# Delta rule of a hybrid decoder layer: preparation inside the projection, samples and end as pipelines

## What is computed

```python
# x: 512 prompt tokens and 8 samples of one token; d_model 2048; p: weights
def token_mixers(h, st, p, pos0):
    proj = h @ p['w_in']                                   # 2048 x 6400
    pa, pb, pc, pd = jnp.split(proj, [A_COLS, A_COLS + B_COLS, A_COLS + B_COLS + C_COLS], axis=-1)
    a_b, a_c, a_h = jnp.split(pa, 3, axis=-1)              # group A: short gated convolution
    u_ext = jnp.concatenate([st_a, a_c * a_h], axis=1)
    y_a = a_b * causal_dwconv(u_ext, p['conv_a_w'])
    ...                                                    # group B: retention -> y_b
    prev = jnp.concatenate([st_shift[:, None, :], pc[:, :-1]], axis=1)   # group C: delta rule
    xs = pc + (prev - pc) * p['mu_c']
    r, kc, vc, wl, al, gl = jnp.split(xs, ..., axis=-1)
    w = -jax.nn.softplus(-(p['w0'] + jnp.tanh(wl) @ p['w2'])) - 0.5
    decay = jnp.exp(-jnp.exp(w))
    a = jax.nn.sigmoid(p['a0'] + al @ p['a2'])
    gate = jax.nn.sigmoid(gl) @ p['g2']
    kk = hs(kc * p['k_k'])                                 # hs: 8 heads of 64
    kk = kk / jnp.maximum(jnp.sqrt(jnp.sum(kk * kk, axis=-1, keepdims=True)), 1e-12)
    k4 = hs(kc * (1.0 + (a - 1.0) * p['k_a']))
    o_c, new_wkv = wkv7_scan(st_wkv, r4, hs(decay), k4, v4, kk, a4)
    o_c = layernorm_lastdim(o_c, RWKV_GN_EPS) * p['lnx_g'] + p['lnx_b']
    bonus = jnp.sum(r4 * k4 * p['r_k'], axis=-1, keepdims=True) * v4
    y_c = (o_c + bonus) * gate
    d1, d2 = jnp.split(pd, 2, axis=-1)                     # group D: 31 taps, norm, swish
    c = causal_dwconv(concat[st_d, d1 * jax.nn.sigmoid(d2)], p['conv_d_w']) + p['conv_d_b']
    y_d = jax.nn.silu(layernorm_lastdim(c, EPS) * p['ln_d_g'] + p['ln_d_b'])
    y = jnp.concatenate([y_a, y_b, y_c, y_d], axis=-1) @ p['w_out']
```

## Time and profile before

| | us |
|---|---|
| median of 3 runs | 3401.66 |
| lowest and highest of them | 3401.51, 3402.88 |
| the profiled execution | 3402.08 |
| its span | 3400.3 |
| busy in the span: PE, DVE, ACT, POOL | 3176.2, 1144.5, 823.6, 1263.9 |

### The profile page before, as it was taken

How to read it: one execution, slowest core, us unless ns; L and a number is a source line. 1 busy time by engine, 2 the same in 40 slices (tenths; PEclk the granted TensorE clock), 3 DMA queues, 4 the chain that set the end, 5 groups by cost and what they waited for, 6 DMA issues and landing times.

```text
span 3400.3 us, 63387 instructions
## 1 busy us (share of the span) xinstructions
PE 3176.2 (93%) x28930; PEld 3083.9 (91%) x28930; DVE 1144.5 (34%) x1355; ACT 823.6 (24%) x1034; POOL 1263.9 (37%) x520
## 2 busy tenths in 40 slices
PE   6999999999259789999989999999999999999997
PEld 6999999999128679978889999999999999999997
DVE  6417873342756542312322311212121111111123
ACT  5431121222102222311212322222122222222221
POOL 6864444333100024322134344444444444444442
PEclk9999999999579899999999999999999999999998
DMA  6663423223000022366542222222222222222222
GB/s 236 214 188 94 120 80 124 93 94 119 24 15 4 4 104 90 112 206 209 180 160 90 87 92 90 93 94 94 93 89 93 93 94 94 90 91 94 94 94 76
DMA packets 147867, 357.57 MB, mean 105 GB/s; under 512 B 24592, under 2 KB 75024, under 8 KB 145296
## 3 DMA queue, kind: packets, MB, share of 16 engines
q1 hardware_dynamic: 109904, 312.58, 27.6%
q10 hardware_dynamic: 37696, 40.94, 3.8%
HBM read 332.34 MB, written 21.13 MB: 104 GB/s over the span
## 4 chain that ended last, share of the span: by engine, by line
PE 92%; DVE 5%; DMA 1%; ACT 1%; issue 0%; ACTq 0%; SPq 0%; POOL 0%; DVEq 0%
PE gp L1400 81%; PE gp L861 1%; PE mp L861 1%; PE mp L853 1%; PE mp L1201 1%; PE gp L1447 1%; PE mp L1184 1%; DMA work<-in_cache_k 0%; PE mp L1232 0%; PE mp L1213 0%; DVE work L972 0%; DVE work L289 0%; DVE work L997 0%; DVE work L1070 0%; DVE work L1854 0%
## 5 line engine op out<-in xcount | busy, mean ns | idle before, releaser
L1380 POOL TENSOR_TENSOR lo<-raw,hi 128x1024 fp32r<-128x1024 f32 x516 | 1263.7, 2452 | 2093.8 <-ACT hi L1517 2093.4
L1400 PE MATMUL gp<-xh,hi 128*128 128x260 f32 x5120 | 1457.5, 285 | 11.4 <-DVE xl L1777 8.6
L1400 PE MATMUL gp<-xh,lo 128*128 128x260 f32 x5120 | 1450.2, 283 | 0.0
L1400 PE MATMUL gp<-xl,hi 128*128 128x260 f32 x5120 | 1445.9, 282 | 0.0
L1517 ACT ACTIVATE hi<-raw 128x1024 fp32r<-128x1024 f32 x516 | 546.6, 1060 | 2096.0 <-PE gp L1400 2048.1
L1400 PEld LDWEIGHTS gp<-xh,hi 128*128 128x128 f32 x5120 | 967.7, 189 | 22.2 <-issue 18.8
L1400 PEld LDWEIGHTS gp<-xl,hi 128*128 128x128 f32 x5120 | 966.8, 189 | 0.5
L1400 PEld LDWEIGHTS gp<-xh,lo 128*128 128x128 f32 x5120 | 966.9, 189 | 0.0
L1400 PE MATMUL gp<-uh,lo 128*128 128x260 f32 x2048 | 578.7, 283 | 0.0
L1400 PE MATMUL gp<-uh,hi 128*128 128x260 f32 x2048 | 578.3, 282 | 0.0
L1400 PE MATMUL gp<-ul,hi 128*128 128x260 f32 x2048 | 576.6, 282 | 0.0
(11 more groups left out here) (299 smaller groups left out, 2103.2 us busy)
## 6 DMA issues: line engine op xcount, KB each, us to landing
raw<-in_w_up SPq DMA_DIRECT2D x128, 512.0 KB, 3.3
raw<-in_w_down SPq DMA_DIRECT2D x128, 512.0 KB, 3.3
raw<-in_w_in SPq DMA_DIRECT2D x100, 512.0 KB, 3.3
raw<-in_w_k SPq DMA_DIRECT2D x32, 512.0 KB, 3.5
raw<-in_w_v SPq DMA_DIRECT2D x32, 512.0 KB, 4.1
raw<-in_w_out SPq DMA_DIRECT2D x32, 512.0 KB, 3.3
raw<-in_w_q SPq DMA_DIRECT2D x32, 512.0 KB, 5.4
work<-in_cache_k SPq DMA_DIRECT2D x32, 512.0 KB, 6.6
```

The lines of the kernel that those rows point to most:

```text
L1380: nc.gpsimd.tensor_tensor(lo[:, s, :], raw[:, s, :], hi[:, s, :].bitcast(F32), ALU.subtract).then_inc(lo_ready, 1)
L1400: last = nc.tensor.matmul(gp[:, par, h, 0:c1 - c0], w, m[:, c0:c1], start=a, stop=b)
```

## The change

What is moved, added and taken out:

- The order of the tiles: D stays in 0 to 7; then half of A (two channel tiles) in 8 to 13, r and v in 14 to 21, B in 22 to 37, tiles 12, 13 and k of C in 38 to 43, and the other half of A in 44 to 49.
- The token shift is made tile by tile behind its eviction (`c_shift`), in place, with a copy of the last columns into a small buffer `c_last`, from which the state output is stored. r and v are stored shifted.
- The d taps go nine to a tile instead of eight; the samples' part of D goes to units 36 and 37, the norm's mean to 38, its centring to 39, variance 40, scaling 41, product 43. Retention's constants are loaded in one go at unit 44.
- Small products of C go to units 82 to 85, unit-length keys to 88 to 94, decays to 92, keys to 95 to 98. Exclusive decays are no longer computed apart: they are the running ones read one column to the left (`g_sh`), and the third exponential falls away.
- r and v are loaded again, with the samples' states, behind the last unit.
- Samples: two operand buffers and both sets of banks are used in turn, and vector n + 2 is built behind the use of vector n.
- Chunk loop: in its first four rounds each channel tile's bonus is made, with two matmuls in bank set z and four DVE operations; it goes into Y. The loop's scratch stands from column 8T on, in one piece.
- End: no shared norm function; the four tiles' means, variances and roots run in two sets of banks in turn, and scale and bias with the bonus are one operation.

```diff
-D_S, R_S, A_S, B_S, K_S = 0, 8, 16, 28, 44
+D_S, A_S, R_S, B_S, K_S, E_S = 0, 8, 14, 22, 38, 44
 SLOTS = [D0 + GT * (1 - n % 2) + n // 2 for n in range(ND_T)]
+SLOTS += [A0 + GT * ((n + 1) % 3) + n // 3 for n in range(NA_T // 2)]
 SLOTS += [C0 + n for n in (0, 1, 2, 3, 8, 9, 10, 11)]
-SLOTS += [A0 + GT * ((n + 1) % 3) + n // 3 for n in range(NA_T)]
 SLOTS += [B0 + GT * (n % 4) + n // 4 for n in range(NB_T)]
-SLOTS += [C0 + n for n in (4, 5, 6, 7, 12, 13)]
+SLOTS += [C0 + n for n in (12, 13, 4, 5, 6, 7)]
+SLOTS += [A0 + GT * ((n + 1) % 3) + n // 3 for n in range(NA_T // 2, NA_T)]
...
+        def c_shift(dve, x, c, n):
...
+            if n >= 2:
+                dve.wait_ge(S("c_shifted"), n - 1)
+            V.tensor_copy(c_last[:, c, :], x[:, NP - 1:]).then_inc(S("c_diff"), 1)
+            V.tensor_tensor(d[:, 1:NP], x[:, 0:NP - 1], x[:, 1:NP], ALU.subtract).then_inc(S("c_diff"), 1)
+            V.tensor_scalar(d[:, 0:1], x[:, 0:1], -1.0, None, ALU.mult).then_inc(S("c_diff"), 1)
+            V.tensor_tensor(d[:, NP:], c_sh[:, c, :], x[:, NP:], ALU.subtract).then_inc(S("c_diff"), 1)
+            dve.wait_ge(S("c_diff"), 4 * (n + 1))
+            V.scalar_tensor_tensor(out=x, in0=d, scalar=pr("mu_c", c), in1=x, op0=ALU.mult, op1=ALU.add).then_inc(S("c_shifted"), 1)
...
+        def c_square(dve, lane, j):
...
+            dve.wait_ge(S("c_shifted"), 8 + 2 + j + 1)
+            lane.done(nc.vector.tensor_scalar(c_kk[:, j, :], c_k[:, j, :], pr("k_k", j), None, ALU.mult))
+            lane.tell(nc.vector.tensor_tensor(c_d[:, j % 2, :], c_kk[:, j, :], c_kk[:, j, :], ALU.mult), S("c_kksq"), j + 1)
...
+            dve.wait_ge(S("c_kkn"), j + 1)
+            lane.done(nc.vector.tensor_scalar(d, d, 1e-12, None, ALU.max))
+            lane.done(nc.vector.reciprocal(d, d))
+            nc.vector.tensor_tensor(c_kk[:, j, :], c_kk[:, j, :], d, ALU.mult).then_inc(S("c_unit"), 1)
...
+            lane.done(nc.vector.tensor_scalar(d, c_a[:, j, :], -1.0, pr("k_a", j), ALU.add, ALU.mult))
+            lane.done(nc.vector.scalar_tensor_tensor(out=c_k[:, j, :], in0=d, scalar=1.0, in1=c_k[:, j, :], op0=ALU.add, op1=ALU.mult))
+            lane.tell(nc.vector.tensor_tensor(c_a[:, j, :], c_a[:, j, :], c_kk[:, j, :], ALU.mult), S("c_vectors"), j + 1)
...
-            if u == 41:
+            if u == 38:
                 d_mean(pe)
...
                 b_pe(pe, h, step)
+            if 82 <= u < 86:
+                c_lora(pe, u - 82)
+            if 89 <= u < 93:
+                c_norm(pe, u - 89)
...
+            if u % 2 == 0 and R_S < u // 2 <= B_S:
...
-                act.wait_ge(evac, evicted(R_S + m))
+                act.wait_ge(S("c_shifted"), m + 1)
...
+            if u == 44:
...
+                act.wait_ge(S("c_shifted"), 8)
+                for t, n in ((b_cos, "cos"), (b_sin, "sin"), (wk(in0 + 8248, 512), "dmat"), (wk(in0 + 8760, 512), "qdec"),
+                             (wk(in0 + 9272, 512), "kdec"), (wk(in0 + 7224, 1024), "sel")):
...
+            if u == 80:
+                act.wait_ge(S("c_shifted"), 8 + 2)
+                nc.scalar.activation(c_lo[0:64, 0, :], c_lo[0:64, 0, :], ACT.Tanh).then_inc(S("c_act0"), 1)
+                nc.scalar.activation(c_sg, c_sg, ACT.Sigmoid).then_inc(S("c_act0"), 1)
...
+            if u == 94:
+                act.wait_ge(S("c_decay"), GT)
+                nc.scalar.activation(c_ld[:, :, NP:], c_ld[:, :, NP:], ACT.Exp).then_inc(S("c_sw"), 1)
...
-            if 8 <= u < 8 + TAPS:
-                d_taps(dve, GT * (u - 8), GT * (u - 7))
-            if u in (39, 40):
...
+            if 8 <= u < 36:
+                d_taps(dve, 9 * (u - 8) // 2, min(9 * (u - 7) // 2, GT * TAPS))
+            if u in (36, 37):
...
+            if u % 2 and (R_S <= u // 2 < B_S or K_S <= u // 2 < E_S):
+                n = u // 2
+                dve.wait_ge(evac, evicted(n))
+                c_shift(dve, target(n), SLOTS[n] - C0, n - R_S if n < B_S else 8 + n - K_S)
...
+            if u == 88:
+                c_square(dve, lane, 0)
+                c_square(dve, lane, 1)
+            if u in (90, 91):
+                c_unit(dve, lane, u - 90)
+                c_square(dve, lane, u - 88)
+            if u in (93, 94):
+                c_unit(dve, lane, u - 91)
+            if u == 92:
+                c_decay(dve, lane)
+            if 95 <= u < 99:
+                c_keys(dve, lane, u - 95)
...
+            if R_S <= n < B_S:
                 dve.wait_ge(S(f"stored{n % 2}"), 16 * ((2 * KT + n - R_S) // 2 + 1))
...
+        c_r, c_v = wk(0, GT, T), wk(4 * T, GT, T)
...
-        cs_S, cs_p, cs_e = (wk(in0 + 2048 * n, NS * GT, 64) for n in range(3))
...
+        cs_p, cs_S = wk(W0, NS * GT, 64), wk(W0 + 5120, NS * GT, 64)
+        cs_e = tuple(wk(W0 + off, NS * GT, 64) for off in (2048, 7168))
...
-        GATES, SCALED = ("in", "iv", "ex"), ("kk", "b", "k", "rd", "bc", "kc", "eg")
+        GATES, SCALED = ("in", "iv"), ("kk", "b", "k", "rd", "bc", "kc", "eg")
...
             act.dma_start(cs_S, A["st_wkv"]).then_inc(S("c_st_loaded"), 16)
...
+            for t, c in ((c_r, 0), (c_v, 8)):
+                act.dma_start(t, pt[:, c:c + GT, :]).then_inc(S("c_again"), 16)
...
             for n in range(5):
...
-                    last = nc.tensor.matmul(mp[:, q, :], blk[:, :], wk(in0 + 4096 + 512 * q, 512), start=True, stop=True)
+                    last = nc.tensor.matmul(w_banks[n % 2][:, q, :], blk[:, :], cs_e[n % 2][:, 8 * q:8 * q + 8, :], start=True, stop=True)
...
-            wkv_ticks(main, lambda i: None)
-            norm_pe(pe, "c", blk, c_o, c_t, False)
...
+            def with_bonus(i, z, step):
+                main(i, z, step)
+                if step == 6 and i < GT:
+                    pe.wait_ge(S("c_rk"), i + 1)
+                    for n, (c0, c1) in enumerate(two_halves):
+                        last = nc.tensor.matmul(w_banks[z][:, 1 + 2 * n, 0:H2], blk[:, :], c_lo[:, 0, c0:c1], start=True, stop=True)
+                    last.then_inc(S("c_rks"), 1)
...
+            pe.wait_ge(S("norm_src"), 2)
+            mean(0)
+            mean(1)
+            var(0)
+            pe.wait_ge(S("norm_xc"), base("c", "xc") + 1)
+            mean(2)
+            var(1)
+            pe.wait_ge(S("norm_xc"), base("c", "xc") + 2)
+            mean(3)
+            for j in range(2):
+                pe.wait_ge(S("norm_std"), base("c", "std") + j + 1)
+                var(2 + j)
+            pe.wait_ge(S("norm_xc"), base("c", "xc") + GT)
+            gate(0)
+            gate(1)
+            pe.wait_ge(S("norm_std"), base("c", "std") + GT)
+            gate(2)
+            gate(3)
...
-            for n, vec in enumerate((c_kk, c_exc, c_a, c_k, c_r)):
-                lane.tell(V.tensor_tensor(e4, e2, by_seq(vec), ALU.mult), S("c_e"), n + 1)
...
+                if n == 4:
+                    dve.wait_ge(S("c_again"), 32)
...
+                lane.tell(V.tensor_tensor(cs_e[n % 2].rearrange(four_d, b=NS), e2, by_seq(vec), ALU.mult), S("c_e"), n + 1)
+
+            build(0)
+            build(1)
+            dve.wait_ge(S("c_st_loaded"), 16)
+            for n in range(5):
...
+                if n + 2 < 5:
+                    build(n + 2)
...
+            def with_bonus(i, z, step):
+                main(i, z, step)
+                if step == 4 and i < GT:
+                    if i:
...
+                    V.scalar_tensor_tensor(out=c_lo[:, 0, :], in0=c_r[:, i, :], scalar=pr("r_k", i), in1=c_k[:, i, :],
+                                           op0=ALU.mult, op1=ALU.mult).then_inc(S("c_rk"), 1)
+                if step == 7 and i < GT:
+                    dve.wait_ge(S("c_rks"), i + 1)
+                    for n, (c0, c1) in enumerate(two_halves):
+                        V.tensor_tensor(Y[:, 8 + i, c0:c1], w_banks[z][:, 1 + 2 * n, 0:H2], c_v[:, i, c0:c1], ALU.mult).then_inc(S("c_bonus"), 1)
+                if step == 9 and i < GT:
+                    dve.wait_ge(S("c_bonus"), 3 * i + 2)
+                    V.tensor_scalar(Y[:, 8 + i, :], Y[:, 8 + i, :], pr("lnx_b", i), None, ALU.add).then_inc(S("c_bonus"), 1)
...
-            norm_dve(dve, lane, "c", c_o, c_t, 64, False)
...
+                dve.wait_ge(S("norm_mean"), base("c", "mean") + j + 1)
+                V.scalar_tensor_tensor(out=halves(c_o[:, j, :]), in0=w_banks[j % 2][:, 0:2, 0:H2], scalar=-1.0 / 64,
+                                       in1=halves(c_o[:, j, :]), op0=ALU.mult, op1=ALU.add).then_inc(S("norm_xc"), 1)
...
+            def scale(j):
+                dve.wait_ge(S("norm_std"), base("c", "std") + j + 1)
+                lane.done(V.reciprocal(c_t[:, j, :], c_t[:, j, :]))
+                lane.done(V.tensor_tensor(c_o[:, j, :], c_o[:, j, :], c_t[:, j, :], ALU.mult))
+                V.scalar_tensor_tensor(out=c_o[:, j, :], in0=c_o[:, j, :], scalar=pr("lnx_g", j), in1=Y[:, 8 + j, :],
+                                       op0=ALU.mult, op1=ALU.add).then_inc(S("c_sum"), 1)
...
+            center(0)
```

(6 more changed lines are left out.)

368 lines of the change are left out of this document (165 added, 203 removed).

## The result

The changed kernel takes 3309.89 us, median of 4 runs (3307.64 to 3314.9), against 3401.59 for the kernel before: a ratio of 0.9733 with a 95% interval of 0.9721 to 0.9745, so 91.7 us less. The forecast was 3315.0. The profiled execution has a span of 3307.1 us, 93.2 less than before.

What follows compares the result with a forecast made beforehand. PE is busy through the projection; the 360.2 us hole behind it is mostly paced by DVE or a DVE–PE–ACT relay. Hole 113.5 us shorter, projection 26.4 longer: 87.1 off 3402.1 gives 3315, range 3293 to 3338.

Steps and rivals of the forecast that it cites:

- preparation's rest: Between last projection product and first broadcast: 8.5 us left of 80.9, with 2.5 us of DVE arrears; saves 72.4.
- samples' step: Five samples' builds and spreads in the hole: overlapping them takes 64.3 us to 39, saving 25.
- chunk loop grows by: Chunk loop in the hole: the added bonus work costs 6.5 us, floor 3.7, ceiling 11.3.
- end: Norms to first w_out product: 53.3 us becomes 30.7, DVE alone setting the pace; saves 22.6.
- hole shorter by: Stretch from last projection product to first w_out product, 360.2 us: 113.5 us shorter in sum.
- wait before the mean: Projection, unit 38: PE waits 10 us for DVE's samples' sums, then loses 2.9 to a lowered clock.
- constants: Retention's constants, asked for at unit 44, wanted at 47: covered by about 1 us; a miss costs 3.
- wait before the fourth product: Projection, unit 92: PE waits 4 us for DVE's fourth block of squares, plus 1.5 for the clock.
- projection longer by: Projection pays 26.4 us for moved PE work, the two waits and the clock behind them; bounds 15 and 37.
- second case: Projection waits mostly covered, 3 us in all without clock dip, and samples at full clock: 3293; chance 0.18.
- third: DVE–GpSimd lock dearer: doubled projection waits, 9 us arrears, loop at ceiling; or samples not overlapped: 3340; chance 0.2.
- fourth case: Slower than before: DVE holds up GpSimd's conversions, so PE starves for low halves in every unit: 3411; chance 0.02.

Runs made afterwards that it cites:

- all_three: Changed kernel with group-D mean and fourth block product each one unit later, and first two operands built ahead of group A's last convolution: 3292.60 us.
- late_fourth: Changed kernel with the fourth block product and its root one unit later, behind unit 93 in place of 92: 3307.06 us.
- both_late: Changed kernel with the fourth block product and the group-D mean each one unit later: 3296.10 us.
- serial_samples: Changed kernel with each of the five broadcast operands built only after the use of the one before: 3334.04 us.
- serial_end: Changed kernel with the end's four tiles one after the other, bonus and gates as changed: 3325.01 us.
- no_bonus: Changed kernel with the bonus left out of the chunk loop, both matmuls and DVE operations: 3303.41 us.
- late_mean: Changed kernel with the group-D mean behind unit 39 in place of 38, and PE's wait for constants at unit 50 in place of 47: 3301.35 us.
- quarter_lo: Changed kernel with each GpSimd conversion to low parts in four operations of 256 columns: 3302.72 us.
- best: Changed kernel with fourth block product and mean each one unit later, first two operands built earlier, and conversions in halves: 3284.35 us.

## Why the prediction was right

Point by point, in the order of its terms, with the profiled executions' numbers.

| term | forecast | measured |
|---|---|---|
| preparation's rest | 8.5 | 6.5 |
| samples' step | 39 | 37.8 |
| chunk loop grows by | 6.5 | 8.7 in this trace (9.3 between the same instructions), 5.4 without the clock's part |
| end | 30.7 | 30.2 |
| hole shorter by | 113.5 | 115.3 |
| PE work moved ahead | 8.0 | 7.8 (4 x 1.08 and 4 x 0.88) |
| wait before the mean, clock behind it | 10, 2.9 | 6.9, 1.5 |
| constants | none, thin cover | 1.2 |
| wait before the fourth product, clock | 4, 1.5 | 4.9, 3.0 |
| projection longer by | 26.4 | 25.8 |

**The hole.** The terms held to within 2 us each but for the loop. Preparation's rest is 2 us shorter because there were no arrears: DVE stood idle for 1.7 us before the last eviction (I had put 2.5 us of arrears). PE's wait before the fourth product had given it the time; with that wait gone, the last eviction starts 1.4 us late in all_three. The samples' step took 37.8 against 39, which is in part luck: the two visible spreads took 5.8 and 5.4 where 6.3 was taken, since the clock was granted 0.86 and not 0.66, and at a lower clock the same step took 41.3 and 41.4 (late_fourth, both_late), more than the 39.9 of the half-clock working. serial_samples shows that the overlap is its whole gain. The loads were hidden, as the chain has no DMA in it there.

**The loop.** The floor was 3.7 and the ceiling 11.3, the value taken 6.5. Priced by itself it is 5.4 (166.9 against 161.5), nearer the floor, as the argument went. That the profile of the changed kernel shows 8.7 was not foreseen: the clock was granted 0.78 in the loop's first 14 us and 0.98 behind them, where both_late had 0.85 and 1.00.

**The end.** The working from durations (four times 3.41 + 0.73 + 0.7, and what stands around them) gave 30.7 for 30.2. serial_end splits the gain in halves.

**The wait before the mean** is the term that was mis-sized by most, 10 us for 6.9. It was a difference of large sums: DVE busy for 174.7 us and idle for 0.8, done at 457.6, and PE there at 448.4, which is 9.2 and was taken as 10. DVE was busy for 171.1 of 173.0 and done at 454.6, and PE was there at 447.7. So the step that was off is DVE's sum, 3.6 us too large. The number of stops was right: counting the operations that took over 0.2 us more than the shortest of their kind, 32 conversions stopped 32 DVE operations in this stretch before, and 30 stopped 30 after, each conversion one. What differs is which operations are stopped, and what an operation costs. DVE's groups over the stretch, before and after:

```profile
L376 DVE SCALAR_TENSOR_TENSOR work<-work,prm 128x512 f32<-128x512 f32 x118 | 139.7, 1250 | 0.0
```

```profile
L339 DVE SCALAR_TENSOR_TENSOR work<-work,prm 128x512 f32<-128x512 f32 x118 | 126.5, 1136 | 0.0
...
L349 DVE TENSOR_TENSOR work<-work,prm 128x31 f32<-128x31 f32 x32 | 7.7, 320 | 0.0
L393 DVE SCALAR_TENSOR_TENSOR work<-work,prm 128x512 f32<-128x512 f32 x4 | 7.0, 1761 | 0.1
...
L385 DVE TENSOR_TENSOR work<-work 128x8 f32<-128x8 f32 x2 | 2.5, 1266 | 0.0
```

The same 118 taps took 139.7 us and now 126.5, because 23 of them are stopped where it was 28. That is no gain: the stops fall on other operations, two on the samples' 32 products (3.31 us in the earlier trace rows, 7.7 now), two on the convolution of A (L393) and one on its gate (L385). "Two stops less" was right, and priced at 4.3 us; all stops together fell by 5.6, since a few taps came when a conversion was half done and waited 1.5 to 1.9 us in place of 2.15. That is 1.3 of the 3.6 us. The other 2.3 are the work itself. I had added 10.7 us by durations that operations have when they stand alone; in DVE's busy time they count for 8.4, since an operation right behind another starts before that one's end (taps of 0.74 us follow each other at 0.66). The four shifts added 6.3 and not 7.0, gate and convolution 4.0 and not 4.3, and the evictions fell by 1.9 and not 0.6.

**The clock's terms** were the weakest guess. I had 2.9 and 1.5 behind the two waits, it was 1.5 and 3.0 in this execution, and behind the same wait before the mean late_fourth and no_bonus show 3.0 (L311 at 6.65 and 6.63 us), serial_end 3.2 (6.83) and serial_samples 1.5 (5.16). So this one wait leaves the time of an execution uncertain by 1.7 us. The Trainium skill (TensorE: Matmul & The Clock Gate, What's actually happening) says that the point at which the clock changes is not tied to the kernel's own start, so that the same kernel shows different counts of slow matmuls; the traces agree, 5.19 against 6.65 us for the same 16 records behind the same 6.9 us of idle.

**The constants** were called covered with about 1 us to spare. The spare was 1.2 us too small: the loads were asked for at 507.9 and landed at 517.04, the queue of six and a landing of 9.2, while PE had come to the place 1.2 us before. In size it is within what the text gave for a miss.

**The rivals.** The second case (waits covered, 3293) and the third (3340) did not come. late_mean and late_fourth show what the second would have needed: one unit more ahead of each product. The fourth case is far off: POOL's conversions average 2.44 us over the kernel, and PE waited for low parts in the projection in no trace; quarter_lo, with 3.2 us for a unit's conversion, doesn't change that.

That forecast and result lie 5 us apart (6.2 for the profiled execution) is partly luck. Of the 6.2, 3.7 are the stretch behind the hole, which was taken as unchanged and scatters by as much; 1.8 are the hole and 0.6 the projection. Inside these the terms cancel: 3.9 us of loop clock stand against a short step of the samples, and the too long wait before the mean against the constants and the clock behind the fourth product.

## What to carry to other kernels

Work moved under a busy engine is free only until the first instruction there that waits for it: write down for each hand-over the time at which the moved chain ends and the time at which the other engine arrives, and where they meet within a few us give the reader one more unit of slack; both repairs here only move hooks by a unit or so. Where DVE and GpSimd work side by side, try the GpSimd operations in halves, since a DVE operation waits for the rest of the one that runs. It pays where DVE has pauses (DVE's busy time behind the hole fell from 480 to 376 us, the last rows of the first table and of best's) and not where DVE works without one, as at the taps; in time it was worth 9.6 us here, and 3.7 where no engine waited for DVE. To forecast the stops in such a dense stretch, count the GpSimd operations: each stopped one DVE operation, whatever the order. And judge an edit of a few us by its own stretch of the trace: late_fourth gained 7.4 us at its place and 2.8 in the median (5.4 by the ratios).

## What the runs showed of the hardware that was not expected

- The same wait of 6.9 us before the same 16 matmul records was followed by 5.16 and 5.19 us in two executions and by 6.63, 6.65 and 6.83 in three others. The same loop took 166.9 to 170.8 us, the longest behind the shortest samples' steps. The granted clock can fall to 0.97 over 50 us in which PE was busy throughout (late_fourth).
- While DVE worked almost without a pause, each GpSimd conversion stopped exactly one DVE operation, 32 by 32 and 30 by 30, and a small one for as long as a large: 128x8 took up to 2.4 us in place of 0.15.
- A GpSimd subtraction of 128x1024 took 2.44 us, of 128x512 1.38, of 128x256 0.80: two halves cost 0.32 more than the whole, four quarters 0.76 more. DVE's busy time fell by 131 and 187 us over the kernel for 142 and 323 more on GpSimd.
- With whole conversions a few of the taps wait long (median 741 ns, longest 2906), with quarters more than half of them wait a little (median 1220, longest 1315): the number of meetings rises as their length falls, and the sum of the taps goes from 127.9 us by 127.8 with halves to 116.5.
